# Rotary halves of a two-layer block exchanged by DMAs from ScalarE's queue instead of a TensorE rotation matrix

## Chip, cores and metric

One core of a Trainium2 chip runs the kernel. The metric is the device time in microseconds (us) of one execution; lower is better. Everything is float32, with weights and the activations that meet them split into a rounded high part and the rest.

## What is computed

Two language-model blocks run one behind the other on 256 tokens of width 1024, each with two layers. The change touches only the first block, whose mixer has three branches: retention (4 heads, with rotary positions on its queries and keys), a gated recurrence (8 heads), and differential attention (8 heads of 2 x 64, also with rotary positions). The first block works on 272 tokens (16 meta tokens ahead of the 256). The rotary step is this part of the reference:

```python
def rope(x, pos):
    d = x.shape[-1]
    inv = ROPE_THETA ** (-jnp.arange(0, d, 2, dtype=F32) / d)
    ang = pos.astype(F32)[:, None] * inv[None, :]
    cos = jnp.cos(ang)[None, :, None, :]
    sin = jnp.sin(ang)[None, :, None, :]
    x1, x2 = jnp.split(x, 2, axis=-1)
    return jnp.concatenate([x1 * cos - x2 * sin, x2 * cos + x1 * sin], axis=-1)
...
q = rope(q, pos)                                   # retention, d = 128
k = rope(k, pos) * RET_DK ** -0.5
...
q = rope(q.reshape(b, l, 2 * DA_HEADS, DA_DH), pos)  # differential attention, d = 64
k = rope(k.reshape(b, l, 2 * DA_HEADS, DA_DH), pos)
```

So with features in partitions, `rope(x) = x * cos + swapped(x) * sin`, where `swapped` exchanges the two halves of each d features and negates one of them.

## The kernel before

Activations are kept feature-major: 128 features in the partitions, 272 tokens along the free dimension. All weights lie in DRAM as one long stream of slabs; a slab is eight 128 x 128 blocks, 512 KB, and goes through a ring of six slots. SyncE loads slab k when TensorE has released its slot (L1975). ScalarE rounds it into `ring_hi` (`feed`, L874), four slabs ahead of the product that it stands at. VectorE, or GpSimd for the slabs in `POOL_SLABS`, subtracts to get `ring_lo` (`low`, L1284 and L1953), three or four slabs ahead. A product of one 128-feature output tile takes one slab: eight blocks, each with three matmuls (high x high, high x low, low x high), 24 matmuls that accumulate in one of eight PSUM banks.

The stages of one layer of the first block, in order: norm; 32 projected tiles of the recurrence (`TILES_HG`); the **fill stage**; 8 gate tiles of retention (`TILES_RG`); retention and differential attention mixed with the branch products; output product; feed-forward.

The fill stage is where the change lies. The recurrence of head h (h = 0 to 7) needs much small work on VectorE (`hg_weights`, `hg_differences`, `hg_factors`, `normalise`), and the five tiles of `TILES_FILL` that are projected beside each head fill TensorE meanwhile. Three of the five are tiles with rotary positions (kinds `rq`, `rk`, `dq`, `dk`; I call them A, B and C) and two hold values (`rv`, `dv`; V1 and V2). There are 24 rotary tiles in a layer and 48 in all: heads 0 and 1 have retention tiles only, head 2 has two of them and one of attention, heads 3 to 7 have attention tiles. Each engine's order is written out in the program:

- **TensorE** (`project_all`, `turn`): projection of a tile, then `turn` of the tile before it. For a rotary tile `turn` is one matmul of a 128 x 128 rotation matrix from the constants (`rotR` or `rotD`) with the tile that was copied to SBUF; for a values tile it is three transposes (L525). Behind tile C comes the output product of head h, behind V2 a sum of squares, then the level products of head h + 1.
- **ScalarE** (`stage`): waits for a projection in PSUM and copies it to one of two slots of `XS` (L861, then a drain at L936), then rounds a slab (`feed`, L874). A slot is free again when VectorE has `taken` the tile of two tiles before. Ahead of tile C of head h stands `exp_levels(h + 1)`, three exponentials on 128 x 1024, 128 x 1088 and 128 x 144 elements. VectorE's `hg_factors(h + 1)` (L1323) waits for them.
- **VectorE** (`settle`): `x * cos` (L1408), wait for the turned tile in PSUM, `turned * sin` (L1410), a drain, the sum (L1413), and a fence that signals `taken`. In head h its order is: low part of a slab, `hg_weights(h)` (L1331 first), low part, `hg_differences(h + 1)` (L1315), `normalise` of head h - 1, low part, `settle(A)`, `hg_factors(h + 1)`, low part, `settle(B)`, low part, `settle(C)`, low part.

In head 7 there is no `hg_differences`, `exp_levels` or `hg_factors` for a next head.

Of the kernel before, what the change touches and what calls it, by code (L numbers as in the profile page):

```python
# [34 lines left out]
P = 128  # L35
# [45 lines left out]
_at = 0  # L81
for _name, _n in [("ones", P), ("invM", 1), ("eps", 1), ("one", 1), ("cosR", T1), ("sinR", T1), ("cosD", T1), ("sinD", T1), ("rotR", P), ("rotD", P), ("rotM", P),
                  ("retD", RET_HEADS * T1), ("lvl", 6 * P), ("causal", 3 * P), ("ident", P),
                  ("ones64", P), ("restart", T1)]:
    CONST[_name] = (_at, _n)
    _at += _n
# [24 lines left out]
def constants():  # L111
# [3 lines left out]
    def put(name, a):  # L115
        at, n = CONST[name]
        c[:a.shape[0], at:at + n] = a.reshape(a.shape[0], n)
# [15 lines left out]
    put("cosR", np.cos(angles(128, 1)))  # L133
    put("sinR", np.sin(angles(128, 1)))
    put("cosD", np.cos(angles(64, 2)))
    put("sinD", np.sin(angles(64, 2)))
    put("rotR", rotation(128, [0]))
    put("rotD", rotation(64, [0, 64]))
    put("rotM", rotation(32, [MLA_NOPE]))
# [75 lines left out]
def program(nc, x_meta, w, par1, lb, lam, final1, par2, positions, final2, consts, out, known):  # L215


    with ExitStack() as ctx:
# [46 lines left out]
        def const(name, shape=None):  # L265
# [8 lines left out]
        cosR, sinR, cosD, sinD = const("cosR"), const("sinR"), const("cosD"), const("sinD")  # L274
        rotR, rotD, rotM = const("rotR"), const("rotD"), const("rotM")
        ident, ones, ones64 = const("ident"), const("ones"), const("ones64")
# [45 lines left out]
        VT = {"h": (HV, 0), "r": (RV, 32), "d": (DV, 64)}  # L322
        ROT = {"rq": (RQ, cosR, sinR, rotR), "rk": (RK, cosR, sinR, rotR),
               "dq": (DQ, cosD, sinD, rotD), "dk": (DK, cosD, sinD, rotD)}

# [97 lines left out]
        def signals(section, names):  # L423
# [5 lines left out]
        s2 = signals("two", "sq total rs normal hn hnlo evac cqn ckn krn qm km oc sg gated gz gez gl gcum zdiff zexp z att sqo normed "  # L429
                     "sc expd w tr o relu used y sigm sigf ff x os gls yb")  # L430
        sm = signals("middle", "sq total rs x")
        se = signals("end", "x")
        b0 = b1 = b2 = bm = Banks(psum, bank_full, bank_free, known.setdefault("banks", {}))

        def enter(stage, layer=0):
            b0.stage, now["layer"], now["stage"] = (stage, layer), layer, stage
            for x in [*s1.values(), *s2.values()]:
                x.layer = layer
# [4 lines left out]
        def _(pe):  # L443
# [120 lines left out]
            def turn(key):  # L564

                kind, h = key
                if kind in ROT:
                    pe.wait_ge(*s1["staged"].upto(key))
                    scores(b1, (kind, h, "turned"), [(slice(0, P), slice(0, T1), ROT[kind][3], XS[:, s1_slot[key], :])])
                elif kind in VALUES:  # L570
                    pe.wait_ge(*s1["staged"].upto(key))
# [287 lines left out]
        def _(act):  # L859
# [20 lines left out]
            def feed(b, key, ahead=4):  # L880
                feed_to(b.slab(key) + ahead)
# [33 lines left out]
            def stage(key):  # L915
# [14 lines left out]
                else:  # L930
# [4 lines left out]
                    op(XS[:, s1_slot[key], :], ps, ACT.Copy, b1.free(key))  # L935
                    nc.scalar.drain().then_inc(*s1["staged"].done(key))  # L936
                feed(b1, key)

            def token_major_values(key):
# [319 lines left out]
        def _(dve):  # L1259
# [141 lines left out]
            def settle(key):  # L1401

                kind, h = key
                if kind in ROT:
# [3 lines left out]
                    V.tensor_tensor(TMP[:, 0, :], x, cos, ALU.mult)  # L1408
                    dve.wait_ge(*b1.full((kind, h, "turned")))
                    V.tensor_tensor(TMP[:, 1, :], b1.of((kind, h, "turned"))[:, 0:T1], sin, ALU.mult)\  # L1410
                        .then_inc(*b1.free((kind, h, "turned")))
                    V.drain()
                    V.tensor_tensor(dst[:, h, :], TMP[:, 0, :], TMP[:, 1, :], ALU.add)  # L1413
                    fence(s1["taken"].done(key))
# [689 lines left out]
```

## Time and profile before

| | |
|---|---|
| median of 3 runs | 2647.0 us (2641.87 to 2649.25) |
| the profiled execution, its own time | 2645.58 us |
| its span, first to last instruction | 2643.8 us |
| busy: TensorE / VectorE / ScalarE / GpSimd | 94% / 69% / 51% / 16% of the span |
| mean granted TensorE clock | 0.962 of full speed |
| DMA, mean over the span | 139 GB/s |
| fill stage of layer 0 / layer 1 | about 125 to 326 us / 918 to 1118 us |

Busy time of matmuls overlaps, since they are pipelined: a matmul is shown with some 290 ns, while in a steady stream the next one starts about 0.13 us behind it. So the cost of a matmul is read from the distance between starts and not from its own length. The "chain that ended last" follows the execution back from its last instruction, at each step to whatever released it.

### The profile page before, as it was taken

To read this page: it belongs to the slowest core of one execution; us is meant where nothing else is said; L and a number is where in the kernel's file an instruction comes from. 1 tells how busy PE (TensorE), PEld (TensorE's weight loads), DVE (VectorE), ACT (ScalarE), POOL (GpSimd) and SP (SyncE) were. 2 spreads that over 40 slices of the span, in tenths; PEclk is the share of its full clock that TensorE was granted. 3 is DMA by queue.
4 is the path that set the end of the run, shared out by engine and by line. 5 is a ranking of instruction groups with operands and counts; after the bars stand their busy time and mean duration, and the time that the engine had idled before them with its cause. 6 is when DMAs were issued, how large, how long until landed. Compare 5 with 4: busy or idle time off the path is not lost.

```text
span 2643.8 us, 50577 instructions
## 1 busy us (share of the span) xinstructions
PE 2495.9 (94%) x19014; PEld 2378.7 (90%) x19014; DVE 1818.4 (69%) x3451; ACT 1354.7 (51%) x2232; POOL 419.3 (16%) x548
## 2 busy tenths in 40 slices
PE   7999998999999999998989997999999989999998
PEld 7999997898999999997889997988999989889998
DVE  6698856666865698856767765676767557667674
ACT  5555555745545655556845545445543454454443
POOL 0000004527920000004618900000000000000000
PEclk9999998999999999998999998788999998899999
DMA  5433342344454433342344553332545532234553
GB/s 212 152 112 104 113 143 88 112 145 146 170 170 160 152 112 104 118 146 89 112 152 152 174 178 119 104 104 103 177 159 183 185 141 100 89 121 143 186 184 134
DMA packets 100433, 366.77 MB, mean 139 GB/s; under 512 B 11632, under 2 KB 12144, under 8 KB 99824
## 3 DMA queue, kind: packets, MB, share of 16 engines
q1 hardware_dynamic: 100208, 363.69, 40.0%
q8 instruction: 151, 2.47, 0.4%
q14 instruction: 74, 0.61, 0.1%
HBM read 362.60 MB, written 1.05 MB: 138 GB/s over the span
## 4 chain that ended last, share of the span: by engine, by line
PE 64%; DVE 15%; POOL 9%; ACT 4%; DVEq 3%; issue 3%; DMA 1%; ACTq 1%; SPq 0%; POOLq 0%
PE psum L449 63%; POOL ring_lo L1953 9%; DVE ring_lo L1284 4%; DMA ring<-w 1%; ACT arena L861 1%; DVE arena L1315 1%; DVE arena L1323 1%; ACT ring_hi L874 1%; PE psum L525 1%; DVE arena_r L1272 1%; DVEq L1264 1%; DVE arena L1413 1%; DVE arena_r L1270 1%; DVE arena L1334 1%; DVE arena L1331 0%
## 5 line engine op out<-in xcount | busy, mean ns | idle before, releaser
L449 PE MATMUL psum<-hn_hi,ring_hi 128*128 128x272 f32 (+2 forms) x3920 | 1171.1, 300 | 50.5 <-DVE ring_lo L1284 20.6
L449 PE MATMUL psum<-hn_hi,ring_lo 128*128 128x272 f32 (+2 forms) x3920 | 1139.9, 292 | 0.0
L449 PE MATMUL psum<-hn_lo,ring_hi 128*128 128x272 f32 (+2 forms) x3920 | 1102.2, 289 | 0.0
L449 PEld LDWEIGHTS psum<-hn_hi,ring_hi 128*128 128x128 f32 x3920 | 770.5, 197 | 83.0 <-issue 59.0
L874 ACT ACTIVATE ring_hi<-ring 128x1024 fp32r<-128x1024 f32 x684 | 715.0, 1056 | 229.1 <-DMA ring<-w 197.8
L1284 DVE TENSOR_TENSOR ring_lo<-ring,ring_hi 128x1024 fp32r<-128x1024 f32 x548 | 667.6, 1228 | 231.7 <-ACT ring_hi L874 194.4
L449 PEld LDWEIGHTS psum<-hn_hi,ring_lo 128*128 128x128 f32 x3920 | 770.1, 196 | 0.0
L449 PEld LDWEIGHTS psum<-hn_lo,ring_hi 128*128 128x128 f32 x3920 | 747.6, 194 | 1.6
L861 ACT ACTIVATE arena<-psum 128x272 f32<-128x272 f32 (+6 forms) x720 | 251.3, 366 | 741.8 <-PE psum L449 632.4
L1953 POOL TENSOR_TENSOR ring_lo<-ring,ring_hi 128x256 fp32r<-128x256 f32 x544 | 419.1, 807 | 1104.8 <-ACT ring_hi L874 1104.7
L449 PE MATMUL psum<-arena_r,ring_hi 128*128 128x256 f32 (+2 forms) x2996 | 554.8, 286 | 14.4 <-DVEq L1264 10.1
L449 PEld LDWEIGHTS psum<-arena_r,ring_hi 128*128 128x128 f32 x2996 | 466.7, 190 | 17.5 <-DVEq L1264 10.9
L449 PE MATMUL psum<-arena_r,ring_lo 128*128 128x256 f32 (+2 forms) x1498 | 425.8, 284 | 0.0
L449 PE MATMUL psum<-arena 128*128 128x128 f32 (+15 forms) x1888 | 280.9, 295 | 23.9 <-ACTq L1021 12.0
L449 PEld LDWEIGHTS psum<-arena 128*128 128x128 f32 (+8 forms) x1888 | 209.7, 169 | 87.2 <-issue 25.5
L449 PEld LDWEIGHTS psum<-arena_r,ring_lo 128*128 128x128 f32 x1498 | 284.2, 190 | 0.0
L861 ACT ACTIVATE arena<-arena 128x272 f32<-128x272 f32 (+8 forms) x161 | 89.3, 574 | 39.4 <-DVEq L1264 33.6
L1272 DVE TENSOR_TENSOR arena_r<-arena,arena_r 128x256 fp32r<-128x256 f32 (+3 forms) x182 | 93.8, 516 | 14.6 <-issue 1.3
L861 ACT ACTIVATE arena<-psum,par_sb 128x272 f32<-128x272 f32 (+1 forms) x88 | 49.8, 568 | 102.6 <-PE psum L449 102.6
L861 ACT ACTIVATE arena<-arena,small 128x128 f32<-128x128 f32 (+1 forms) x128 | 59.4, 464 | 70.2 <-DVEq L1264 69.2
L1270 DVE CAST arena_r<-arena 128x256 fp32r<-128x256 f32 (+3 forms) x182 | 70.3, 386 | 15.9 <-issue 0.8
L861 ACT ACT_TABLE_LOAD x58 | 74.4, 1283 | 3.5 <-PEq L2098 0.7
(152 smaller groups left out, 1601.7 us busy)
## 6 DMA issues: line engine op xcount, KB each, us to landing
ring<-w SPq DMA_DIRECT2D x684, 512.0 KB, 3.3
cst<-consts SPq DMA_DIRECT2D x1, 2120.0 KB, 14.5
x_sb<-x_meta SPq DMA_DIRECT2D x1, 1088.0 KB, 4.9
out<-x_sb SPq DMA_DIRECT2D x1, 1024.0 KB, 4.8
arena<-lam SPq DMA_DIRECT2D x1, 256.0 KB, 4.0
par_sb<-par SPq DMA_DIRECT2D x1, 193.0 KB, 4.8
pos_sb<-positions SPq DMA_DIRECT2D x1, 128.0 KB, 6.3
cst<-consts SPq DMA_DIRECT2D x1, 65.5 KB, 4.9
```

Of the source, the lines that this page charges most:

```text
L449: i = nc.tensor.matmul(out_, lhsT=lhsT, rhs=rhs, start=first, stop=last)
L525: t = nc.tensor.transpose(ps[rows, cols], src, ident[0:src.shape[0], 0:src.shape[0]])
L861: i = nc.scalar.activation(out_, in_, func, **kw)
L874: nc.scalar.activation(ring_hi[:, slot], ring[:, slot], ACT.Copy).then_inc(slab_hi[k % RING], 1)
L1264: i = V.drain()
L1270: V.tensor_copy(hi, src)
L1272: return V.tensor_tensor(lo, src, hi.bitcast(F32), ALU.subtract)
L1284: V.tensor_tensor(ring_lo[:, slot], ring[:, slot], ring_hi[:, slot].bitcast(F32), ALU.subtract)\
L1315: V.tensor_tensor(zq[:, z, 0:n].rearrange("p (b t s) -> p b t s", t=2, s=s), paired(C, s, n // (2 * s), step + s), paired(C, s, n // (2 * ...
L1323: V.tensor_tensor(d, d, paired(k, s, n // (2 * s), step + s), ALU.mult)
L1334: V.tensor_tensor(Lt[:, 0:3, :], Lt[:, 0:3, :], Lt[:, 3:6, :], ALU.add)
L1953: i = nc.gpsimd.tensor_tensor(ring_lo[:, part], ring[:, part], ring_hi[:, part].bitcast(F32), ALU.subtract)
```

## The change

The constants `rotR` and `rotD` go (256 columns of `cst`), `turn` does nothing for rotary tiles, and the sign moves into the sine tables. Behind each copy of a rotary tile, ScalarE waits for its own copy's signal and issues DMAs that write the exchanged halves straight into the destination tile `dst`: two of 64 partitions for a retention tile, four of 32 partitions for an attention tile, each 272 floats wide. They signal a semaphore of their own for each `XS` slot. VectorE waits for that one instead of for a PSUM bank, multiplies `dst` by the signed sine in place and adds `x * cos`. In all 16 retention tiles x 2 and 32 attention tiles x 4, 160 DMAs.

```diff
-    put("sinR", np.sin(angles(128, 1)))
+    half = lambda d: np.where(np.arange(P) % d < d // 2, -1.0, 1.0)[:, None]
+    put("sinR", half(128) * np.sin(angles(128, 1)))
     put("cosD", np.cos(angles(64, 2)))
-    put("sinD", np.sin(angles(64, 2)))
-    put("rotR", rotation(128, [0]))
-    put("rotD", rotation(64, [0, 64]))
+    put("sinD", half(64) * np.sin(angles(64, 2)))
     put("rotM", rotation(32, [MLA_NOPE]))
...
-        ROT = {"rq": (RQ, cosR, sinR, rotR), "rk": (RK, cosR, sinR, rotR),
-               "dq": (DQ, cosD, sinD, rotD), "dk": (DK, cosD, sinD, rotD)}
+        ROT = {"rq": (RQ, cosR, sinR, P), "rk": (RK, cosR, sinR, P), "dq": (DQ, cosD, sinD, P // 2), "dk": (DK, cosD, sinD, P // 2)}
...
+        exchanged = list(signals("exchanged", "first second").values())
...
                 kind, h = key
-                if kind in ROT:
-                    pe.wait_ge(*s1["staged"].upto(key))
-                    scores(b1, (kind, h, "turned"), [(slice(0, P), slice(0, T1), ROT[kind][3], XS[:, s1_slot[key], :])])
-                elif kind in VALUES:
+                if kind in VALUES:
...
                     op(XS[:, s1_slot[key], :], ps, ACT.Copy, b1.free(key))
                     nc.scalar.drain().then_inc(*s1["staged"].done(key))
+                    if kind in ROT:
+                        exchange_halves(key)
                 feed(b1, key)
+
+            def exchange_halves(key):
+
+                kind, h = key
+                dst, _, _, d = ROT[kind]
+                act.wait_ge(*s1["staged"].upto(key))
+                for at in range(0, P, d):
+                    for a, b in ((at, at + d // 2), (at + d // 2, at)):
+                        nc.scalar.dma_start(dst[a:a + d // 2, h, :], XS[b:b + d // 2, s1_slot[key], :])\
+                            .then_inc(*exchanged[s1_slot[key]].done(key, 16))
...
                     x = XS[:, s1_slot[key], :]
                     V.tensor_tensor(TMP[:, 0, :], x, cos, ALU.mult)
-                    dve.wait_ge(*b1.full((kind, h, "turned")))
-                    V.tensor_tensor(TMP[:, 1, :], b1.of((kind, h, "turned"))[:, 0:T1], sin, ALU.mult)\
-                        .then_inc(*b1.free((kind, h, "turned")))
+                    dve.wait_ge(*exchanged[s1_slot[key]].upto(key))
+                    V.tensor_tensor(dst[:, h, :], dst[:, h, :], sin, ALU.mult)
                     V.drain()
-                    V.tensor_tensor(dst[:, h, :], TMP[:, 0, :], TMP[:, 1, :], ALU.add)
+                    V.tensor_tensor(dst[:, h, :], dst[:, h, :], TMP[:, 0, :], ALU.add)
                     fence(s1["taken"].done(key))
```

ScalarE's order in a head with attention tiles, from tile A's copy to tile C's (`ring_hi` rows are `feed`, the three rows on 4x256, 1088 and 144 elements are `exp_levels`, the rows 128x2x128 and 16x128 copy the turned values tile). Before:

```order
L861 ACTIVATE arena<-psum 128x272
L874 ACTIVATE ring_hi<-ring 128x1024
L861 ACTIVATE arena<-psum 128x2x128
L861 ACTIVATE arena<-psum 16x128
L861 ACTIVATE arena<-psum 128x272
L874 ACTIVATE ring_hi<-ring 128x1024
L861 ACTIVATE arena<-arena 128x4x256
L861 ACTIVATE arena<-arena 128x1088
L861 ACTIVATE arena<-arena 128x144
L861 ACTIVATE arena<-psum 128x272
L874 ACTIVATE ring_hi<-ring 128x1024
```

Now:

```order
L857 ACTIVATE arena<-psum 128x272
L944 DMA arena<-arena 32x272 x4
L870 ACTIVATE ring_hi<-ring 128x1024
L857 ACTIVATE arena<-psum 128x2x128
L857 ACTIVATE arena<-psum 16x128
L857 ACTIVATE arena<-psum 128x272
L944 DMA arena<-arena 32x272 x4
L870 ACTIVATE ring_hi<-ring 128x1024
L857 ACTIVATE arena<-arena 128x4x256
L857 ACTIVATE arena<-arena 128x1088
L857 ACTIVATE arena<-arena 128x144
L857 ACTIVATE arena<-psum 128x272
```

Four DMA issues stand behind each of the two copies, both ahead of the exponentials (two behind each copy for retention tiles).

TensorE's order in the last head of the fill stage, between the last matmul of tile C's projection, the output product of the head (three matmuls on `arena`) and the next projection. Before:

```order
L449 MATMUL psum<-hn_hi,ring_lo 128x272
L449 MATMUL psum<-arena,cst 128x272
L449 MATMUL psum<-arena 128x272
L449 MATMUL psum<-arena 128x144
L449 MATMUL psum<-arena 128x16
```

Now:

```order
L448 MATMUL psum<-hn_hi,ring_lo 128x272
L448 MATMUL psum<-arena 128x272
L448 MATMUL psum<-arena 128x144
L448 MATMUL psum<-arena 128x16
```

The matmul with the rotation matrix (`arena,cst`) is gone; it was 48 times in the program. VectorE has as many instructions as before.

## Rows read from the trace of the kernel before

**Rows 1.** The page: busy time of the engines, and the chain that ended last by engine

```profile
PE 2495.9 (94%) x19014; PEld 2378.7 (90%) x19014; DVE 1818.4 (69%) x3451; ACT 1354.7 (51%) x2232; POOL 419.3 (16%) x548
...
PE 64%; DVE 15%; POOL 9%; ACT 4%; DVEq 3%; issue 3%; DMA 1%; ACTq 1%; SPq 0%; POOLq 0%
```

**Rows 2.** Windows: length, busy us (count) of PE, PEld, DVE, ACT, POOL; PE clock, DMA share, GB/s

```profile
149.20:297.30 148.10, 142.78 (x1133) 134.51 (x1131) 133.67 (x314) 71.57 (x136) 0.00 (x0) 1.00 0.32 107
297.30:326.10 28.80, 28.35 (x226) 27.02 (x227) 20.30 (x37) 15.36 (x29) 0.00 (x0) 1.00 0.33 111
```

**Rows 3.** Waits from 149.2 to 297.3 us: total us, times, longest

```profile
PE psum L525 <- ACTq L936: 4.8, 5, 1.3
...
DVE arena L1413 <- issue: 0.5, 1, 0.5
```

**Rows 4.** Chain in order of time, end of the fill stage in both layers

```profile
297.27 0.40 ACT arena L861
...
307.27 14.70 PE psum L449 x108
...
1099.72 14.70 PE psum L449 x108
```

**Rows 5.** Timeline of TensorE around one rotation: start, length, instruction

```profile
143.07 0.29 PE L449 MATMUL psum<-hn_hi,ring_lo 128*128 128x272 f32 x1
143.20 0.62 PE L449 MATMUL psum<-arena,cst 128*128 128x272 f32 x2
...
143.78 0.29 PE L449 MATMUL psum<-hn_lo,ring_hi 128*128 128x272 f32 x1
143.91 0.29 PE L449 MATMUL psum<-hn_hi,ring_lo 128*128 128x272 f32 x1
```

**Rows 6.** Timeline of ScalarE, head 6 of layer 1 (brackets: idle before, and releaser)

```profile
1074.80 1.07 ACT L874 ACTIVATE ring_hi<-ring 128x1024 fp32r<-128x1024 f32 x1
...
1077.64 0.40 ACT L861 ACTIVATE arena<-psum 128x272 f32<-128x272 f32 x1 [1.24 <-PE psum L449]
...
1079.12 2.25 ACT L861 ACTIVATE arena<-arena 128x1024 f32<-128x1024 f32 x3
```

**Rows 7.** Timeline of VectorE in the same head

```profile
1082.35 0.43 DVE L1410 TENSOR_TENSOR arena<-psum,cst 128x272 f32<-128x272 f32 x1
1082.88 0.44 DVE L1413 TENSOR_TENSOR arena<-arena 128x272 f32<-128x272 f32 x1
1083.44 2.92 DVE L1323 TENSOR_TENSOR arena<-arena 128x256 f32<-128x256 f32 x8
```

**Rows 8.** Timelines in head 0: layer 0 first, then layer 1

```profile
138.99 2.91 DVE L1323 TENSOR_TENSOR arena<-arena 128x256 f32<-128x256 f32 x8 [0.34 <-ACTq L964]
...
929.43 2.26 ACT L861 ACTIVATE arena<-arena 128x1024 f32<-128x1024 f32 x3
...
931.74 2.91 DVE L1323 TENSOR_TENSOR arena<-arena 128x256 f32<-128x256 f32 x8
...
940.59 1.22 DVE L1284 TENSOR_TENSOR ring_lo<-ring,ring_hi 128x1024 fp32r<-128x1024 f32 x1
941.94 1.02 DVE L1331 TENSOR_TENSOR arena<-psum,cst 128x512 f32<-128x512 f32 x2
```

**Rows 9.** SyncE's slab loads in the loop: issue ns min/median/max, and time to landing

```profile
L1975 SPq DMA_DIRECT2D ring<-w x678: 332/333/352, 29.8 to 2615.9; - x170
...
DMA to landing us min/median/max: 3.0/3.3/7.5
```

**Rows 10.** SyncE's issues at the start: one row of the timeline, then size and landing, then the six first slabs

```profile
4.57 0.43 SPq L1966 DMA_DIRECT2D par_sb<-par  x1
...
cst<-consts SPq DMA_DIRECT2D x1, 2120.0 KB, 14.5
...
par_sb<-par SPq DMA_DIRECT2D x1, 27.0 KB, 3.4
...
L1970 SPq DMA_DIRECT2D ring<-w x6: 432/560/1017, 5.5 to 8.9; - x6
```

More of the change, by code:

```diff
@@ L81 @@
 _at = 0
-for _name, _n in [("ones", P), ("invM", 1), ("eps", 1), ("one", 1), ("cosR", T1), ("sinR", T1), ("cosD", T1), ("sinD", T1), ("rotR", P), ("rotD", P), ("rotM", P),
+for _name, _n in [("ones", P), ("invM", 1), ("eps", 1), ("one", 1), ("cosR", T1), ("sinR", T1), ("cosD", T1), ("sinD", T1), ("rotM", P),
                   ("retD", RET_HEADS * T1), ("lvl", 6 * P), ("causal", 3 * P), ("ident", P),
@@ L274, in program @@
         cosR, sinR, cosD, sinD = const("cosR"), const("sinR"), const("cosD"), const("sinD")
-        rotR, rotD, rotM = const("rotR"), const("rotD"), const("rotM")
+        rotM = const("rotM")
         ident, ones, ones64 = const("ident"), const("ones"), const("ones64")
@@ L436, in enter @@
             b0.stage, now["layer"], now["stage"] = (stage, layer), layer, stage
-            for x in [*s1.values(), *s2.values()]:
+            for x in [*s1.values(), *s2.values(), *exchanged]:
                 x.layer = layer
```

## The prediction

> **What bounds the kernel now.** I read the page first. TensorE is busy 94% of the span and holds 64% of the chain [rows 1], which would make every matmul that goes a gain. That is an average over stages, so I went on to the chain in order of time. In the fill stage, where all 48 rotations stand, it is VectorE that holds the chain: from 149.2 to 297.3 us in layer 0 and from 941.9 to 1089.7 us in layer 1, that is heads 1 to 6. The windows show the same from the other side. Of 148.1 us VectorE is busy 133.7 us [rows 2], and what is left are the drains between its dependent instructions: the only wait of an arithmetic instruction on its list is one gap of 0.5 us that no engine ends [rows 3]. TensorE meanwhile waits for ScalarE's copy of tile V1, five times and 4.8 us in all [rows 3]. That copy in turn waits until VectorE has taken tile B. ScalarE is busy half of the stretch [rows 2]. So a head takes some 25 us, whatever TensorE does.
>
> TensorE takes the chain over when V1 of head 6 has been copied [rows 4], and head 7 runs at its pace: 8.65 us, three transposes, then 14.70 us with 108 matmuls in a row, in both layers [rows 4]. Head 0 is its own case. TensorE and VectorE are nearly level there, and head 1's level products arrive a little after VectorE is free [rows 8].
>
> **What goes: 48 rotations.** Without one, matmuls start 0.13 us apart (143.78 to 143.91). Around a rotation, three steps (the rotation, a high-high and a high-low matmul) take from 143.07 to 143.78, 0.71 us [rows 5]; without it the two steps would take 0.26. So a rotation costs 0.45 us, 48 of them 21.6 us. Only those count that lie where TensorE holds the chain:
> - heads 1 to 6, 18 per layer: nothing. TensorE would only wait longer for V1's copy; what is late next is VectorE itself.
> - head 7, three per layer, inside the 108 matmuls [rows 4]: 3 x 0.45 = 1.35 us per layer, 2.7 us in both. Behind it comes a stage at TensorE's pace.
> - head 0, three per layer: TensorE would deliver 1.35 us earlier, but VectorE can use little. Its low part ends at 940.59 + 1.22 = 941.81 and the next instruction starts at 941.94 [rows 8]; neighbours overlap a little, so I take 0.2 us per layer, for layer 0 too.
>
> **What VectorE pays.** Three tensor_tensor on 128 x 272 before, three now, in the same order with the same drain. The sine product reads SBUF twice instead of PSUM and SBUF: 0.43 us for the old form, 0.44 for the sum, the nearest row of the new one [rows 7]; 0.5 us over 48 at most. I take zero.
>
> **What ScalarE pays.** The issue of a DMA occupies its instruction stream. No DMA is issued from ScalarE before, so the price d has to be bounded. SyncE's slab loads take 0.333 us each in the loop [rows 9]; at the start a small load takes 0.43 us and six slab loads issued back to back 0.56 us in the median, up to 1.02 [rows 10]. I take d = 0.33, the steady row, and keep 0.03 (hardly more than a register instruction) and 1.02 as the ends. The wait for its own copy comes on top; the drain that it waits for was there already, and I estimate w = 0.1 us from the gaps of 0.04 to 0.1 that the chain calls issue.
>
> The Trainium skill, page "DMA: Bandwidth & Descriptors", section "Anatomy of one DMA", puts the sequencer's dispatch at about 50 ns of a DMA's roughly 2 us, for another issuing path; SyncE's 0.333 us disagree, as far as the two are the same thing. By that figure head 0 would pay nothing and the sum below would be -2.7 us instead of -1.6; I go by the row.
>
> An attention tile costs ScalarE 4d + w = 1.42 us, a retention tile 2d + w = 0.76. Who waits for it is `hg_factors(h + 1)` on VectorE, by way of `exp_levels`. In heads 3 to 6, the ones with attention tiles only:
> - A's issues stand ahead of the copy of B, which waited 1.24 us for TensorE [rows 6]; 1.42 - 1.24 = 0.18 is left.
> - B's issues add 1.42, so the exponentials end 1.60 us later. They ended at 1079.12 + 2.25 = 1081.37 and VectorE asks for them at 1083.44 [rows 6, 7]: 2.07 us of slack, the smallest of these heads. Cost nothing. The cover breaks when 2(4d + w) - 1.24 = 2.07, at d = 0.39.
>
> Head 0 has retention tiles and no such slack. In layer 1 the exponentials end at 931.69 and VectorE starts at 931.74; in layer 0 it waits 0.34 us for them already [rows 8]. B's 0.76 us come through: 0.76 and 0.71, less the 0.2 us in which VectorE waited later anyway. **Cost: 0.56 + 0.51 = 1.1 us.** Heads 1 and 2 pay 0.76 out of slack of over a microsecond. `feed` is moved back by the same 1.4 us at most; its slabs are rounded four ahead, and the low part that needs one comes a tile later. Copies of V1 and V2 have no issues ahead of them but those of C, and wait for VectorE anyway. The values' transposes, GpSimd and SyncE's queue are not passed by anything.
>
> **The wait that is added.** VectorE now waits for the exchange, with `hg_factors`, the low parts and so TensorE's next weights queued behind it. The copy of A is done at 1074.80, and VectorE needs the exchange at 1082.35 [rows 6, 7]: 7.5 us later. A DMA took from issue to landing 3.3 us in the median with 512 KB, 7.5 at most [rows 9], and 3.4 with 27 KB [rows 10]. With 1.4 us for the issues that makes 4.8 us; 2.7 are spare. In head 0 a retention tile is staged some 5 us ahead, and needs 0.76 + 3.4 = 4.2. I take zero, with 0 and 7.5 us for the landing as ends. The exchanges add 139 KB to the 512 KB per tile while the DMA engines are busy a third of the time [rows 2], and the constants shrink by 131 of 2120 KB [rows 10] in a load that is not on the chain.
>
> **Sum:** -2.7 + 1.1 = -1.6 us. Against the profiled execution's own 2645.58 us (span 2643.8) that makes 2644.0; the median of the runs shown is 1.4 us above it, so I forecast 2645.4. A difference under 0.3% (7.9 us) is no change.
>
> **Rivals.**
> - *ScalarE's issues come out on the chain* (slower). If d is that of the back-to-back issues, 0.56 us, the exponentials of heads 3 to 6 end 2(2.34) - 1.24 = 3.44 us later, 1.37 past the slack, eight times: 11 us. Head 0 costs 2 x 1.22 - 0.4 - 0.05 = 2.0. With -2.7 that is +10.3: 2657 us. For: attention tiles issue four in a row, and SyncE's grew when it did so [rows 10]. Against: those six stood behind nine other DMAs, and the steady 0.333 varies by 0.02 only [rows 9]. It passes +0.3% from d = 0.53 on. At d = 0.43 it is +1.3 us.
> - *The exchange lands late* (slower). If landing takes 7.5 us instead of 3.4, A and C, which VectorE takes some 7 us behind their copies, are each about 1.4 us late in heads 2 to 6: 10 x 1.4 x 2 = 28 us, 2673 us. A sharper form is that the four DMAs go one behind the other, 3.4 us each: over 13 us for a tile, and far above 2700. The skill's same page, "Rules for kernel authors", says that two transfers to disjoint partition halves serialize, as they share all the engines. Against both: the load issued at 4.57 us, behind seven others from the same queue, landed 3.4 us later [rows 10], which it could not have done behind them one by one.
> - *All rotations count* (faster). Were TensorE the bound throughout, as its 94% say, 21.6 us would go and 2625 us be left. Against: VectorE's unbroken chain in rows 2 and 3.
> - *The change does not do what it says*: the order of instructions shows 48 matmuls gone and 48 groups of DMAs added, so this has no chance of its own.
>
> **Chances.** Forecast, with every d up to 0.5: 0.80. ScalarE's issues above that: 0.12. Late exchange: 0.03. TensorE's saving counts: 0.05. So faster 0.05, same 0.80, slower 0.15. The forecast's own range, with the spread of the runs (2641.87 to 2649.25), is 2641 to 2650. To reach 8 in 10 with some margin for d, I stretch the upper end to the first rival's price: 2641 to 2658.
>
> **What would show it.** Right: the fill stage still takes VectorE's chain from head 1 to 6 with 25.2 us per head; TensorE's waits for L936 grow from 4.8 us by some 0.45 x 3 us per head; the last PE piece shrinks from 14.70 to 13.3 us; issues on ScalarE of 0.33 us; `hg_factors` waits 0.7 to 1.1 us in head 0 and nowhere else; no wait at the sine product in heads 1 to 6. Wrong: issues of over 0.5 us with VectorE waiting for the exponentials in heads 3 to 6, or VectorE waiting for a DMA at the sine product, or heads that got shorter than 25 us.

## The result, and the profile after

| | before | changed |
|---|---|---|
| median of 4 runs beside each other | 2644.43 us (2638.17 to 2649.25) | 2680.33 us (2675.28 to 2683.7) |
| the profiled execution, own time / span | 2645.58 / 2643.8 us | 2675.28 / 2673.5 us |
| mean granted TensorE clock | 0.962 | 0.952 |

The ratio is 1.0136, with an interval of 1.0107 to 1.0164: some 36 us slower, where 2645.4 us and a range of 2641 to 2658 were predicted. The profiled execution is the fastest of the four, so its own difference is 29.7 us.

The page hardly shows it: busy times are those of before [rows 1], less 96 matmul instructions (two for each rotation). New in the chain is ACTq, the waiting and issuing on ScalarE's instruction stream, with 5% where it had 1%.

```profile
PE 2497.8 (93%) x18918; PEld 2380.0 (89%) x18918; DVE 1818.1 (68%) x3451; ACT 1353.4 (51%) x2232; POOL 419.8 (16%) x548
...
PE 65%; DVE 10%; POOL 9%; ACT 5%; ACTq 5%; issue 2%; DVEq 2%; DMA 1%; SPq 0%; POOLq 0%
```

Line L944 of the changed kernel is the exchange. Its duration is what it holds ScalarE's stream for, in ns (min/median/max); the last line is issue to landing:

```profile
L944 ACTq DMA_DIRECT2D arena<-arena x160: 468/612/1482, 134.3 to 1145.6; - x160
...
  DVE arena L1418: 1.5, 4
...
DMA to landing us min/median/max: 1.8/2.7/5.2
```

So an issue costs 0.61 us, against 0.33 taken from [rows 9]. The transfers themselves are no trouble: L1418, the sine product, waited 1.5 us for them in the whole program. ScalarE's timeline in an attention head of layer 0, from tile A's copy to V1's (compare [rows 6]):

```profile
268.29 2.44 ACTq L944 DMA_DIRECT2D arena<-arena  x4
...
272.55 0.40 ACT L857 ACTIVATE arena<-psum 128x272 f32<-128x272 f32 x1 [0.17 <-issue]
273.06 2.44 ACTq L944 DMA_DIRECT2D arena<-arena  x4
...
276.51 2.25 ACT L857 ACTIVATE arena<-arena 128x1024 f32<-128x1024 f32 x3
...
279.43 2.44 ACTq L944 DMA_DIRECT2D arena<-arena  x4
...
285.06 0.40 ACT L857 ACTIVATE arena<-psum 128x272 f32<-128x272 f32 x1 [1.52 <-DVEq L1272]
```

Four issues are 2.44 us. Tile B's copy no longer waits for TensorE (0.17 us, by "issue"; it was 1.24). The exponentials end at 276.51 + 2.25 = 278.76, and `hg_factors` (L1331 now) starts at 278.82, late:

```profile
220.09 2.90 DVE L1331 TENSOR_TENSOR arena<-arena 128x256 f32<-128x256 f32 x8 [1.98 <-ACTq L972]
249.94 2.90 DVE L1331 TENSOR_TENSOR arena<-arena 128x256 f32<-128x256 f32 x8 [3.19 <-ACTq L972]
278.82 2.90 DVE L1331 TENSOR_TENSOR arena<-arena 128x256 f32<-128x256 f32 x8 [2.62 <-ACTq L972]
308.42 2.90 DVE L1331 TENSOR_TENSOR arena<-arena 128x256 f32<-128x256 f32 x8 [3.06 <-ACTq L972]
```

Starts are 29.9, 28.9 and 29.6 us apart; before it was 25.2. Of some 4 us per head the brackets explain 2 to 3. The rest is in the waits from 151.5 to 315 us (line waited for, total us, times, longest), where TensorE's waits for V1's copy, L524 now, have grown from 4.8 us and 1.3 at most [rows 3]:

```profile
PE psum L524 <- ACTq L932: 16.8, 5, 4.5
...
DVE arena L1331 <- ACTq L972: 11.4, 5, 3.2
```

and in what TensorE does behind such a wait, first on its timeline, then in windows of 2 us (columns as in [rows 2], the clock is the third number from the end):

```profile
226.81 0.90 PE L524 MATMUL psum<-cst,arena 128*128 128x128 f32 x3 [4.34 <-ACTq L932]
```

```profile
227.00:229.00 2.00, 2.00 (x8) 1.47 (x7) 1.81 (x5) 1.00 (x2) 0.00 (x0) 0.50 0.00 0
...
235.00:237.00 2.00, 2.00 (x17) 2.00 (x18) 1.60 (x5) 0.36 (x2) 0.00 (x0) 1.00 0.03 8
```

TensorE stood idle for 4.34 us, then worked at a granted clock of 0.50, its level of 1.2 GHz, and from 235 us on at 2.4 GHz again. The chain shows what hangs on that: the piece of 78 matmuls from V1's transposes to the copy of tile A. First the one that the chain of the kernel before shows (ahead of the 14.70 in [rows 4]), then six of the changed kernel:

```profile
298.30 8.65 PE psum L449 x78
```

```profile
174.29 10.17 PE psum L448 x78
200.17 8.66 PE psum L448 x78
227.71 11.15 PE psum L448 x78
257.78 9.97 PE psum L448 x78
286.44 10.91 PE psum L448 x78
315.98 9.89 PE psum L448 x78
```

Five of six are 1.2 to 2.5 us too long, 8.8 us in all. The slow ones stand behind idle gaps of TensorE of 2.3 us (the first of them, V1 of head 1) and of 4.1 to 4.5 us (V1 of heads 3 to 6); behind the gaps of 1.4 and 1.5 us in heads 0 and 2 the clock stayed at 1.00. From 151.5 to 315 us the mean clock is 0.94 (1.00 before):

```profile
151.50:315.00 163.50, 142.69 (x1094) 134.19 (x1092) 134.78 (x315) 72.34 (x136) 0.00 (x0) 0.94 0.35 112
```

The heads now run in a loop: V1's copy, TensorE's piece of 78 matmuls, ScalarE's list from tile A's copy to the exponentials, `hg_factors` and tile B on VectorE, the next V1's copy. So my theory was: the issues make the exponentials late, which makes V1 late, which lets TensorE idle so long that its clock falls, which makes the next tile A, and so ScalarE's list, later still. The rivals were the traffic or the landing of the DMAs, and TensorE missing the rotations' matmuls as work.

### The profile page after: what moved, and what is told of

The parts are those of the page before. It is cut to its first block, busy times and chain, and to the rows that moved or that the text cites. A ratio compares the mean times of both kernels' runs of the same rounds, so it can differ in the third digit from the quotient of the medians.

```text
span 2673.5 us, 50497 instructions
## 1 busy us (share of the span) xinstructions
PE 2497.8 (93%) x18918; PEld 2380.0 (89%) x18918; DVE 1818.1 (68%) x3451; ACT 1353.4 (51%) x2232; POOL 419.8 (16%) x548
## 4 chain that ended last, share of the span: by engine, by line
PE 65%; DVE 10%; POOL 9%; ACT 5%; ACTq 5%; issue 2%; DVEq 2%; DMA 1%; SPq 0%; POOLq 0%
PE psum L448 64%; POOL ring_lo L1960 9%; ACT arena L857 2%; ACTq L944 2%; ACT ring_hi L870 2%; DVE ring_lo L1292 2%; DVE arena L1331 1%; DMA ring<-w 1%; ACTq L972 1%; PE psum L524 1%; DVE small L1477 0%; ACTq L932 0%; ACT L857 0%; DVE arena_r L1280 0%; DVEq L1272 0%
## 5 line engine op out<-in xcount | busy, mean ns | idle before, releaser
L448 PE MATMUL psum<-arena_r,ring_hi 128*128 128x256 f32 (+2 forms) x2996 | 555.2, 286 | 13.2 <-DVEq L1272 10.1
L448 PE MATMUL psum<-arena 128*128 128x128 f32 (+15 forms) x1888 | 294.1, 304 | 23.1 <-ACTq L1149 11.8
L448 PEld LDWEIGHTS psum<-arena 128*128 128x128 f32 (+8 forms) x1888 | 220.6, 177 | 89.5 <-issue 28.6
L1280 DVE TENSOR_TENSOR arena_r<-arena,arena_r 128x256 fp32r<-128x256 f32 (+3 forms) x182 | 93.8, 515 | 14.6 <-issue 1.3
L524 PE MATMUL psum<-cst,arena 128*128 128x128 f32 (+3 forms) x288 | 50.7, 279 | 45.2 <-ACTq L932 45.1
L524 PEld LDWEIGHTS psum<-cst,arena 128*128 128x128 f32 (+3 forms) x288 | 31.9, 131 | 55.6 <-ACTq L932 48.7
## 6 DMA issues: line engine op xcount, KB each, us to landing
cst<-consts SPq DMA_DIRECT2D x1, 1992.0 KB, 13.9
```

What stands on the lines that cost most here:

```text
L448: i = nc.tensor.matmul(out_, lhsT=lhsT, rhs=rhs, start=first, stop=last)
L524: t = nc.tensor.transpose(ps[rows, cols], src, ident[0:src.shape[0], 0:src.shape[0]])
L1280: return V.tensor_tensor(lo, src, hi.bitcast(F32), ALU.subtract)
```

## The experiments

### Only the DMAs, or only their time

`e1_both` keeps every rotation and adds the DMAs; their result is overwritten. VectorE waits for them before it writes the sum.

```diff
                     nc.scalar.drain().then_inc(*s1["staged"].done(key))
+                    if kind in ROT:
+                        exchange_halves(key)
...
                     V.drain()
+                    dve.wait_ge(*exchanged[s1_slot[key]].upto(key))
                     V.tensor_tensor(dst[:, h, :], TMP[:, 0, :], TMP[:, 1, :], ALU.add)
```

> The kernel before, with the exchange DMAs added on ScalarE's queue behind each copy (VectorE waits for them before its sum, and overwrites what they wrote); the 48 rotations stay and give the result. My theory (ScalarE's issues of 0.6 us each make exp_levels late, and TensorE's longer wait for V1's copy lowers its clock): as slow as the change or slower by the rotations of head 7, 2680 to 2686 us, hg_factors waits 2 to 3 us for the exponentials in heads 3 to 6, and the fill stage shows stretches at half clock. Rival (it is the missing TensorE work that lets the clock fall): no half clock in the fill stage, 2655 to 2662 us. Rival (the DMAs cost nothing, VectorE's new form or the new banks do): 2645 us.

`e7_filler` has no DMA at all. ScalarE copies a constant tile to scratch instead, for about the same time.

```diff
+                    if kind in ROT:
+                        for _ in range(2 if kind[0] == "r" else 5):
+                            op(scr[:, :], cosR, ACT.Copy)
+                            nc.scalar.drain()
```

> The kernel before, with no DMA at all: behind each copy of a rotary tile ScalarE copies 128 x 272 constants to a scratch tile, five times for attention tiles (about 2.5 us, as four issues took) and twice for retention tiles (1.0 us). My theory (ScalarE's time is what counts, whatever it is spent on): within 8 us of e1, 2672 to 2688 us, with the same waits for the exponentials and the same half clock. Rival (traffic or landing of the exchange DMAs matters): 2645 to 2655 us.

Measured beside a kernel before of 2644.76 us: `e1_both` 2674.99 us, ratio 1.0115 (1.0084 to 1.0147); `e7_filler` 2672.53 us, 1.0115 (1.0078 to 1.0152). ScalarE's timeline in `e7_filler`, then the wait of its `hg_factors` for the exponentials in the whole program (24.7 us, 12 times, in the changed kernel):

```profile
265.97 2.44 ACT L862 ACTIVATE scr<-cst 128x272 f32<-128x272 f32 x5
```

```profile
  ACTq L969: 20.4, 10
```

Copies that take ScalarE's time without moving a byte by DMA cost the same 28 us as the DMAs with the rotations kept (30 us). That excludes traffic, landing and the missing matrix work as the main cause; 2.44 us on ScalarE's list, three times a head, is enough. `e1_both` is a few us below its expected range and below the changed kernel. With the rotations kept, TensorE's gaps ahead of V1 are shorter in its trace: 2.4 to 2.8 us in heads 3 to 6 instead of 4.1 to 4.5, and 1.0 instead of 2.3 us in head 1. So the missing matrix work has a part, but how large it is was not tested by itself. Behind gaps of some 2.4 us the clock fell in one head and not in another: in `e7_filler` it did so in heads 3 to 5 of layer 0 and only in head 6 of layer 1.

### Which tiles

`e9_retention_only` and `e10_attention_only` exchange only the tiles of the one kind by DMA; the others keep matrix and unsigned sine. The line that chooses, for `e9_retention_only` (it is `"d"` in the other):

```diff
-                    if kind in ROT:
+                    if kind[0] == "r" and kind in ROT:
                         exchange_halves(key)
```

> Only the 16 retention tiles (heads 0 to 2) are exchanged by DMAs from ScalarE, two each; the 32 attention tiles keep their rotation matrix. Theory (price of an issue 0.6 us, two per tile, 1.2 to 1.3 us): head 0 of each layer pays 1.3 us less some tenths, heads 1 and 2 have slack, the changed kernel's own trace stands 2.8 us later at head 0's exponentials in layer 0 and 1.0 us in layer 1: +3 to +5 us, 2646 to 2650 us. Rival (any DMA issue on ScalarE costs the same share of the loss, so 32 of 160 issues cost a fifth of 36 us): +7 us, 2650 to 2653 us.

> Only the 32 attention tiles (heads 2 to 7) are exchanged by DMAs from ScalarE, four each; the 16 retention tiles keep their rotation matrix. Theory (four issues of 0.6 us ahead of the exponentials, twice, overrun the 2.07 us of slack, and TensorE falls to its lower clock behind longer waits): nearly the whole loss of the change is here, +30 to +35 us, 2673 to 2679 us. Rival (a fifth of the loss is retention's, by the count of issues): 2670 to 2672 us.

Beside 2643.03 us before: retention only 2649.93 us, ratio 1.0028 (1.0016 to 1.0041); attention only 2676.09 us, 1.0125 (1.0105 to 1.0146). So +7 and +33 us. The 128 issues of the attention tiles carry most of it, as they should when slack decides. Retention came out at the upper edge of my range, where the rival by count was as good; its trace tells more. In head 0 the cost comes by the mechanism that the prediction gave. Head 0 of layer 0 (138.99 before [rows 8]) and then of layer 1:

```profile
140.30 2.92 DVE L1339 TENSOR_TENSOR arena<-arena 128x256 f32<-128x256 f32 x8 [1.51 <-ACTq L980]
...
934.92 2.92 DVE L1339 TENSOR_TENSOR arena<-arena 128x256 f32<-128x256 f32 x8 [1.31 <-ACTq L980]
```

That is 2.5 us more waiting. The second place is head 2. Ahead of V1 of head 1 TensorE has a gap of 2.34 us, and behind it the lower clock; the third line is the same gap in `e1_both`, with the rotations:

```profile
172.24 0.55 PE L526 MATMUL psum<-cst,arena 128*128 128x128 f32 x3 [2.34 <-ACTq L939]
```

```profile
172.79 10.16 PE psum L450 x78
```

```profile
172.00 0.55 PE L526 MATMUL psum<-cst,arena 128*128 128x128 f32 x3 [1.02 <-ACTq L937]
```

The gap is 2.33 us in `e5_gpsimd` (below) as well, where ScalarE issues nothing: in this head it is the missing rotations that lengthen it. The piece takes 10.16 us in both layers, `hg_factors` of head 2 waits 0.22 and 0.60 us for the exponentials and starts 0.7 us later in each layer. The profiled execution is 3.4 us longer than that of the kernel before; for the rest of the 7 us between the medians there is no trace.

### The price of an issue

`e6_prices` is the kernel before with four DMAs of 32 x 272 floats from SBUF to SBUF on SyncE, in the form of an attention tile's, and four small loads from DRAM moved to ScalarE's start.

```diff
+            sp.wait_ge(consts_in, 16)
+            for at in range(0, P, 32):
+                sp.dma_start(scr[at:at + 32, :], cst[at ^ 32:(at ^ 32) + 32, NFIRST:NFIRST + T1]).then_inc(scr_in, 16)
...
+            nc.scalar.dma_start(lb_sb, lb).then_inc(params_in, 16)
```

> The kernel before, two prices only: at the start four of the small parameter loads (DRAM to SBUF, 128 rows) are issued by ScalarE instead of SyncE, and SyncE issues four SBUF to SBUF DMAs of 32 x 272 into a scratch tile, of the exchange's form, ahead of its loop. If the engine sets the price: ScalarE's loads take about 0.6 us each and SyncE's exchanges 0.33 to 0.43. If the form (SBUF to SBUF, 32 rows) sets it: ScalarE's loads 0.43 and SyncE's exchanges 0.6.

SyncE's timeline in the middle of its list, and ScalarE's at its start:

```profile
23.30 2.47 SPq L1976 DMA_DIRECT2D scr<-cst  x4
```

```profile
0.75 0.41 ACTq L1027 DMA_DIRECT2D arena<-lb  x1
```

On SyncE too the four take 2.47 us, 0.59 each without the gaps between them, while ScalarE issues three of its loads from DRAM in 0.41 to 0.46 us (the fourth took 0.70). Between these two engines the price goes with the form of the transfer, SBUF to SBUF here, and not with the engine that issues it. One thing is not separated, since the exchanges always come in groups: in the changed kernel's chain the first issue of a group takes 0.47 to 0.52 us and those behind it mostly 0.61. So a single one of them would still cost more than 0.33, but part of the 0.61 may come from standing in a row.

### Out of the exponentials' way

`e2_behind_exp` issues tile B's exchange behind `exp_levels` instead of ahead of it.

```diff
                             exp_levels(h + 1)
+                            exchange_halves(later.pop())
```

> The change, with only tile B's exchange moved: it is issued behind exp_levels(h + 1) instead of ahead of it, in heads 0 to 6. My theory: the exponentials end at most 1.3 us later than before in attention heads, inside 2.07 us of slack, so hg_factors does not wait, TensorE's wait for V1 stays near 1 us, no half clock: 2641 to 2648 us. Rival (the exchanges cost by their number or traffic wherever they stand): over 2665 us. Rival (TensorE's clock falls for want of the rotations): hg_factors does not wait and still half clock in the fill stage, 2650 to 2665 us.

A miss: 2658.65 us, ratio 1.0049 (1.0031 to 1.0066). `hg_factors` waited 2.9 us in the whole program, so that wait was removed. But ScalarE's timeline shows the next thing in its place:

```profile
241.76 2.45 ACTq L947 DMA_DIRECT2D arena<-arena  x4
244.31 0.40 ACT L857 ACTIVATE arena<-psum 128x272 f32<-128x272 f32 x1 [2.64 <-issue]
244.81 2.49 ACTq L947 DMA_DIRECT2D arena<-arena  x4
...
248.91 0.40 ACT L857 ACTIVATE arena<-psum 128x272 f32<-128x272 f32 x1
```

B's and C's exchanges now stand in a row between the exponentials and V1's copy at 248.91, which starts without idle time before it. VectorE had taken its slot already, in this head by 0.1 us only (its sum ends at 248.79), in the next two by 1.0 and 2.2 us. Twelve issues, 7.3 us per head, are themselves on the loop from V1's copy to V1's copy, and TensorE still waits for V1, 2.5 to 3.8 us in heads 3 to 6. `e11_behind_exp_busy` is the same with 16 matmuls of unused result in TensorE's wait for V1:

```diff
                 if kind in VALUES:
+                    pre = b1.take(pe, (kind, h, "turned"))
+                    if kind != "hi" and not h & 1:
+                        for _ in range(16):
+                            nc.tensor.matmul(pre[:, 0:T1], lhsT=H1[:, 0, 0:P], rhs=H1[:, 0, :], start=True, stop=True)
                     pe.wait_ge(*s1["staged"].upto(key))
```

> The version with tile B's exchange behind the exponentials (2658.7 us before), with sixteen matmuls of unused result ahead of each wait of TensorE for a values tile of an even head (16 x 0.13 = 2.1 us out of a wait of 2.5 us). Theory (a good part of what was left is TensorE's lower clock in the pieces of level products, 10.2 instead of 8.65 us): 2648 to 2655 us. Rival (ScalarE's own list, with twelve issues or 7.3 us per head, is the loop, whatever the clock): 2656 to 2660 us.

2650.51 us, ratio 1.0030 (1.0017 to 1.0042): 7.5 us above the kernel before beside it, where `e2_behind_exp` was 13.9 us above its own. So useless work for TensorE took off some 6 us; the two intervals overlap a little, but the traces show it plainly. The pieces of 78 matmuls, without the extra matmuls and with them:

```profile
249.95 10.18 PE psum L448 x78
276.85 10.16 PE psum L448 x78
```

```profile
248.21 8.66 PE psum L448 x78
274.59 8.66 PE psum L448 x78
```

### The clock in the changed kernel

`e3_dummies` is the changed kernel with 24 such matmuls.

> The change, with 24 extra matmuls of 128 x 272 on TensorE ahead of each wait for V1's copy, about 3 us of its 4.3 us wait; their result is overwritten. My theory on the clock (it falls because TensorE stands idle in that wait): no half clock in the fill stage, its level products take 8.65 us again instead of 9.9 to 11.2, and the time falls by 8 to 18 us, to 2662 to 2672 us, while hg_factors still waits for the exponentials. Rival (the half clock there is unrelated to the wait): the same half-clock stretches, 2680 us or more.

2672.48 us, ratio 1.0104 (1.0071 to 1.0136), 8 us below the changed kernel. The intervals of the ratios overlap, but the slowest of its four runs (2673.93) is below the fastest of the changed kernel (2675.28). The clock from 149.2 to 297.3 us is 0.99, with one slow piece left; in the heads of layer 1 it is 1.00, and there the starts of `hg_factors` are 27.0 us apart:

```profile
1056.17 2.91 DVE L1335 TENSOR_TENSOR arena<-arena 128x256 f32<-128x256 f32 x8 [2.07 <-ACTq L976]
1083.19 2.91 DVE L1335 TENSOR_TENSOR arena<-arena 128x256 f32<-128x256 f32 x8 [1.81 <-ACTq L976]
```

That is the issues' own price at full clock: 27.0 - 25.2 = 1.8 us per head. The exponentials' wait stays, as it should. The matmuls cost something where TensorE holds the chain (in head 7 of layer 0 they take 3.01 us of it), so 8 us is too little for what the clock took. That chain, the same head, also shows head 7 as the prediction had it, 13.33 us instead of 14.70, with all of ScalarE's issues in place:

```profile
312.51 8.65 PE psum L448 x78
...
321.49 13.33 PE psum L448 x102
```

### Half the issues

`e4_two_dmas` exchanges attention tiles by two DMAs of 64 partitions too, which leaves their rotary step wrong and the work the same.

```diff
-                dst, _, _, d = ROT[kind]
+                dst, d = ROT[kind][0], P
```

> The change, with two DMAs of 64 partitions for the attention tiles too instead of four of 32, the same bytes: they exchange the halves of 128 features, so the rotary step of differential attention is left wrong. My theory (the price is per issue, about 0.56 us whatever the rows): a tile costs ScalarE 1.15 us, the exponentials end 1.1 us later at most in heads 3 to 6 and fit into 2.07 us of slack: 2643 to 2650 us, no half clock. Rival (bytes or rows set the price): 2670 to 2682 us.

2650.5 us, ratio 1.0027 (1.0015 to 1.0039), half a microsecond above the range. A tile costs mostly 1.12 us, now and then up to 1.59, and `hg_factors` waits 4.8 us in all. "No half clock" was a miss: TensorE's gaps ahead of V1 are 1.5 to 2.6 us in heads 3 to 6, and behind most of them the piece of 78 matmuls takes 10.1 to 10.2 us, so that a good part of what is left must be the clock. Halving the price took off three quarters of the loss, which is what a threshold does and a proportional cost does not.

### Another engine's list

`e5_gpsimd` issues all exchanges from GpSimd, which has nothing to do in the fill stage.

```diff
-                    if kind in ROT:
-                        exchange_halves(key)
...
+            for k in sorted(POOL_SLABS):
+                if k % SLABS1 == 96:
+                    enter("one", k // SLABS1)
+                    for key in TILES_FILL:
+                        if key[0] in ROT:
+                            exchange_halves(key)
```

> The change, with the same exchange DMAs issued from GpSimd, which has nothing else to do in the fill stage. My theory: ScalarE's list is as before, hg_factors never waits for the exponentials; if four issues and the landing fit into the 7.5 us between a tile's copy and VectorE's need, 2641 to 2648 us. Rival (GpSimd issues or lands them too late): VectorE waits at the sine product, each microsecond over 7.5 costs twice per head: 2650 to 2700 us.

2644.74 us beside 2642.02, ratio 1.0009 (0.9999 to 1.0019): the loss is gone. An issue takes GpSimd 0.50 us; VectorE waited for an exchange three times, 5.7 us in all:

```profile
L1951 POOL DMA_DIRECT2D arena<-arena x160: 496/498/660, 134.2 to 1115.5; - x160
...
  DVE arena L1406: 5.7, 3
```

Yet the 2.7 us that the rotations should give in head 7 did not appear. Its chain at the end of layer 0's fill stage shows both why and that the saving is real (V1 of head 6 is turned, level products of head 7, tiles A to C of head 7; before: 8.65 and 14.70 [rows 4]):

```profile
301.71 10.14 PE psum L448 x78
...
312.18 13.34 PE psum L448 x102
```

14.70 - 13.34 = 1.36 us are saved, and 1.49 lost to the lower clock just ahead. TensorE's gaps ahead of V1 in heads 1 to 6 are 2.3 to 2.6 us in eight cases of twelve, where they were 1.3 at most, though ScalarE's list is as before: so it is the missing rotations, 3 x 0.45 us in a head, that make them longer here. So `e8_gpsimd_busy` adds 12 useless matmuls ahead of V1's wait in all heads, and `e12_gpsimd_busy_inner` in heads 1 to 6 only (its line; the other has no `not in`):

```diff
+                    if kind != "hi" and not h & 1 and (kind, h) not in (TILES_FILL[3], TILES_FILL[-2]):
+                        for _ in range(12):
```

> The exchanges issued from GpSimd (2644.7 us before, ratio 1.001), with twelve matmuls of unused result (128 x 272) ahead of each wait of TensorE for a values tile of an even head, into the bank that the transposes then fill. They take some 12 x 0.13 = 1.6 us out of a wait of 2.1 us. Theory (what is left of the rotations' gain was eaten by matmuls at the lower clock behind those waits): the lower-clock stretches of the fill stages go, and the -2.7 us of head 7 come out in full: 2639 to 2642 us. Rival (VectorE bounds the heads, so the clock there costs nothing, and what eats the gain is VectorE's wait for landing exchanges, 5.7 us): 2643 to 2648 us, no change against the version without the extra matmuls.

> As the GpSimd version with twelve extra matmuls ahead of V1's wait, but only in heads 1 to 6; in heads 0 and 7 TensorE does not wait there, so the extra matmuls stood on its path (1.67 and 1.50 us in the trace). Theory: the clock still stays up in the fill stages, the piece behind head 6's level products stays at 13.34 us instead of 14.70, and the time falls by up to 2 x (1.5 + some of 1.67) = 3 to 4 us against the version with the matmuls in all heads: 2640 to 2642 us beside a kernel before of 2643, ratio 0.998 to 1.000, the saving that the prediction gave to head 7. Rival (GpSimd's exchanges cost something elsewhere, in head 0 or at the end of the stage): 2643 to 2646 us.

`e8_gpsimd_busy`: 2644.62 us beside 2643.03, ratio 1.0003 (0.9988 to 1.0018). The clock was 1.00 and the pieces were right, but in head 7 nobody waited for V1, so that the useless matmuls (1.50 us) took the saving's place:

```profile
308.28 13.34 PE psum L448 x102
321.62 1.50 PE psum L570 x12
```

`e12_gpsimd_busy_inner`, where they are gone from heads 0 and 7: 2640.69 us beside 2642.76, ratio 0.9991 (0.9982 to 1.0).

```profile
299.19 8.65 PE psum L448 x78
...
308.18 13.34 PE psum L448 x102
321.51 0.33 PE psum L524 x3
```

That is -2.1 us, the size that the prediction gave the rotations (-2.7), at the edge of what can be measured and far below the 0.3%. It is the only version below the kernel before beside it, apart from the single run of `e6_prices`.

## Why the prediction was wrong, point by point

**Right.** VectorE bounds the heads, so 48 rotations are worth head 7's 1.35 us per layer and no more: the traces show 1.36, and the version that gets the saving and pays nothing else is 2.1 us faster, not 21.6. VectorE's in-place sine product costs nothing (0.43 us before and 0.44 after). The exchange lands in time: 2.7 us in the median, 1.5 us of waiting in all. If four DMAs of a tile went one behind the other, as the Trainium skill, page "DMA: Bandwidth & Descriptors", section "Rules for kernel authors", has it for two transfers to disjoint partition halves, the last would land some 10 us after the first issue at 2.4 us each; issue to landing was 2.4 us in the median for the quarter tiles and 5.2 at most for any exchange, so no serializing that matters shows here. Head 0's mechanism was right too: late exponentials, 1.51 and 1.31 us, with 2d + w now 1.3. (Two sizes were taken in other units than the profile's: the exchanges add 136 KB for each tile and the constants shrink by 128 KB in its units. Nothing hangs on it.)

**The step that failed** is "I take d = 0.33, the steady row". It measured 0.61, just above the rival's 0.56 and on the far side of the cover's break at 0.39 that the text had worked out. SyncE's steady row was of another form, DRAM to SBUF. The nearest rows were the start's issues back to back (0.56), for attention tiles come four in a row too; I discounted them because other DMAs stood ahead, and the chance of 0.12 for d above 0.5 was too low for that reason. The Trainium skill's 50 ns for the sequencer's dispatch, on GpSimd's path (page "DMA: Bandwidth & Descriptors", section "Anatomy of one DMA"), is farther off than any row, as far as it is the same thing: an issue took GpSimd 0.50 us here, and ScalarE and SyncE 0.61 and 0.59.

**The rival's sum was too small as well.** With d = 0.61 its own formula gives 2(2.44 + 0.1) - 1.24 - 2.07 = 1.8 us per head, and `e3_dummies` measured just that, 27.0 - 25.2. Eight heads make 14 us. The changed kernel's trace loses 33.9 - 1.6 = 32.3 us from the start of the first fill stage to the end of the second (the chain has the transposes of head 7's V1 in layer 1 at 1114.42 before and at 1148.31 after; 1.6 us of difference were there ahead of the first stage). By the starts of `hg_factors`:

- heads 3 to 6 of both layers: 26.7 us, that is 3.3 per head. 1.8 of these are the issues; the other 1.5, some 12 us, are **TensorE's lower clock**. The chain says the same head by head: in heads 4 to 6 of layer 0 `hg_factors` starts another 4.7, 3.3 and 4.4 us later than before, and less what V1's transposes and the piece behind them take beyond 0.55 and 8.65 us, 1.8 us are left each time.
- heads 0 to 2: 3.3 us in both layers, against the 1.1 that I gave them: 2.4 us in head 0, 1.4 in head 2 behind the slow piece of 10.2 us that `e9_retention_only` shows too, and half a microsecond won in head 1.
- head 7: +2.3 us in both layers together instead of -2.7. Of these 5.0 us, 4.1 are the lower clock again: ahead of tile A's copy the transposes and the piece take 0.84 and 9.89 us in layer 0, and 0.90 and 10.86 in layer 1, instead of 0.55 and 8.65.

```profile
1122.86 10.86 PE psum L448 x78
...
1144.14 1.48 ACTq L944
```

From A's copy on, head 7 runs on ScalarE's list with its twelve issues, 13.7 us in layer 0 and 14.6 in layer 1 instead of the 15.0 of before at TensorE's pace, so that it still gets most of the rotations' saving; in layer 1 one issue of 1.48 us stands in the way. VectorE waits longer for rounded slabs there, 4.5 us instead of 0.3 in layer 0, but no such wait ends in the chain.

**The second step that failed** is this clock, a term that stood nowhere in the text. The prediction said for heads 1 to 6 "nothing. TensorE would only wait longer for V1's copy", and so costed that wait at nothing. Where TensorE idles for 4.3 us, it comes back at 1.2 GHz, and its next piece stands on the loop, ahead of tile A's copy. The Trainium skill warns of it, and I missed it (page "TensorE: Matmul & The Clock Gate", section "Why this matters for your kernels": no long idle gaps between bursts of matmuls, or the clock goes back down). This case's trace agrees: 8.65 us became 9.9 to 11.2, and with useless matmuls in the gap it was 8.65 again in all heads but one. Added up for the profiled execution, an estimate from the figures above: some 18 us of lower clock (12.5 in heads 3 to 6, 1.4 in head 2, 4.1 in head 7), some 17.5 us of issues (14.2 in heads 3 to 6, 2.4 in head 0, 0.9 for the long one), less the rotations' 2.7 and the half microsecond of head 1.

**What would show it** was put rightly: issues of over 0.5 us with VectorE waiting for the exponentials in heads 3 to 6. It is what came.

**Not settled.** How much of the lower clock goes back to the issues and how much to the missing rotations, which both lengthen TensorE's gaps; the second half of the 7 us of the retention tiles alone; and how the 36 us of the medians split beyond the profiled execution's 30, since only that one has a trace. From the fill stage's end on it won 4 us back, in stages that the change doesn't touch.

## What to carry to other kernels

Before a DMA issue is moved to a computing engine, take its price from an issue of the same form (here SBUF to SBUF, four in a row, 0.6 us each on ScalarE and SyncE), multiply by how many stand ahead of the next thing that someone waits for, and look for the point where the slack breaks; if the price is only bounded and the break lies inside the bounds, the range has to hold what comes behind it. An idle engine's list (GpSimd's here) took the same 160 issues at no cost clear of the noise.

Where TensorE is not the bound, its waits are still not free: look at the granted clock behind the longest of them, and at whether the next matmuls lie on the loop. A wait grown from 1.3 to 4.5 us cost 1.5 us per head, nearly as much again as the 1.8 of the issues. Taking work away from TensorE ahead of such a wait makes it longer as well.

## What the runs showed of the hardware that I had not expected

- The issue of a DMA from SBUF to SBUF with 32 partitions x 272 floats holds ScalarE's and SyncE's streams for 0.61 and 0.59 us, one with 64 partitions 0.56 to 0.59; a load from DRAM took ScalarE 0.41 to 0.46 and SyncE 0.33. GpSimd issued the same exchanges in 0.50 us each, with VectorE busy 132.1 of 148.1 us beside it.
- TensorE's granted clock stood at 0.50 for some us behind an idle gap of 4.3 us, while gaps of up to 1.3 us in the kernel before left it at 1.00 [rows 2, 3]. In the traces of the other runs it stayed at 1.00 behind V1's gaps of up to 1.7 us; behind gaps of 1.9 to 2.6 us it fell in most cases and stayed in others (2.42 us: both in `e7_filler`), and behind longer ones it fell. 12 to 24 matmuls of unused result in the gap kept it at 1.00 but for one piece, and made three of the kernels some 5 to 8 us faster (`e3_dummies`, `e11_behind_exp_busy`, `e12_gpsimd_busy_inner`; 1 us in `e8_gpsimd_busy`, where they stand on the chain in heads 0 and 7).
